# One decoder layer with a mixture of experts: GpSimd's expert loop without its outer branch, and a small copy moved from ScalarE's queue to SyncE's

## What is computed

```python
def hier_moe(h, w_rg, w_re, w_g, w_u, w_d):
    ...                                     # top-1 group of 4, then top-2 of its 8 experts
    order = jnp.argsort(flat_e)             # token-expert pairs, sorted by expert
    ...
    chunk_e = jnp.clip(jnp.searchsorted(pend, ...), 0, N_EXPERTS - 1)
    def expert_chunk(args):
        xc, e = args
        return (jax.nn.silu(xc @ w_g[e]) * (xc @ w_u[e])) @ w_d[e]
    ...
    out = jax.ops.segment_sum(ys.astype(jnp.float32) * slot_w[:, None], slot_tok, num_segments=n + 1)[:n]
```

## Time and profile before

| what | value |
|---|---|
| median of three runs | 1815.52 us (1813.52 to 1822.35) |
| the profiled execution: its time, its span | 1813.52 us, 1811.8 us |
| PE busy | 1439.0 us (79%) |
| PEld busy | 837.5 us (46%) |
| DVE busy | 664.2 us (37%) |
| ACT busy | 371.6 us (21%) |
| POOL busy | 192.8 us (11%) |
| moved by DMA | 336.98 MB, mean 186 GB/s |

### The profile page before, as it was taken

One profiled execution on the slowest core, in us unless ns is written; L12 is line 12 of the kernel. 1 busy time (PEld: TensorE's weight loads), 2 busy tenths in 40 slices (PEclk: granted clock), 3 DMA queues, 4 the chain that ended last, 5 costly groups with the idle time before them and its releaser, 6 DMA issues. The chain is left out here.

```text
span 1811.8 us, 22638 instructions
## 1 busy us (share of the span) xinstructions
PE 1439.0 (79%) x7436; PEld 837.5 (46%) x7436; DVE 664.2 (37%) x1324; ACT 371.6 (21%) x794; POOL 192.8 (11%) x348
## 2 busy tenths in 40 slices
PE   5999999448569978873369990699999999999960
PEld 4665454148535555552235540354454454454430
DVE  3002999941137766653512228011011011011007
ACT  4000011013125555552111110011111111111113
POOL 0000011136110000002300000111111111111111
PEclk7999999769858999996679995799999999999985
DMA  8300000076142000004441100899999999999927
GB/s 319 137 1 6 12 15 18 14 271 190 53 121 71 1 1 1 1 17 130 128 166 49 67 29 2 324 412 412 412 406 413 414 403 413 412 401 409 407 94 285
DMA packets 79756, 336.98 MB, mean 186 GB/s; under 512 B 9770, under 2 KB 41643, under 8 KB 61698
## 3 DMA queue, kind: packets, MB, share of 16 engines
q1 hardware_dynamic: 61866, 287.76, 40.6%
q0 software_dynamic: 15440, 47.30, 7.6%
q10 hardware_dynamic: 2384, 1.06, 0.2%
HBM read 311.20 MB, written 29.45 MB: 188 GB/s over the span
## 5 line engine op out<-in xcount | busy, mean ns | idle before, releaser
L1630 PE MATMUL ps<-arena 128*128 128x512 f32 x544 | 241.1, 600 | 0.0
L1630 PEld LDWEIGHTS ps<-arena 128*128 128x128 f32 x544 | 102.6, 191 | 137.5 <-issue 137.4
L311 PE MATMUL ps<-arena 128*128 128x512 f32 (+3 forms) x432 | 159.0, 528 | 1.3 <-DVE arena L439 1.3
L453 DVE SCALAR_TENSOR_TENSOR arena<-arena 128x1024 f32<-128x1024 f32 x120 | 144.3, 1278 | 0.3
L1331 PE MATMUL ps<-arena 128*128 128x512 f32 (+1 forms) x288 | 129.5, 603 | 15.5 <-DVE arena L1426 15.5
L1684 PE MATMUL ps<-arena 128*128 128x512 f32 x272 | 121.6, 600 | 3.8 <-DMA arena<-scratch_h,ints 3.8
L1638 PE MATMUL ps<-arena 128*64 128x256 f32 x1088 | 121.2, 380 | 0.0
L277 PE MATMUL ps<-arena 128*128 128x352 f32 x384 | 116.1, 465 | 0.4 <-ACT arena L340 0.4
L311 PEld LDWEIGHTS ps<-arena 128*128 128x128 f32 (+1 forms) x432 | 77.3, 180 | 80.8 <-issue 73.7
L935 ACT ACTIVATE arena<-ps,arena 128x640 f32<-128x640 f32 (+7 forms) x128 | 89.9, 702 | 119.9 <-DVE arena L1010 108.5
L848 PE MATMUL ps<-arena 128*128 128x128 f32 x528 | 82.8, 287 | 35.6 <-ACT arena L945 32.0
(11 more groups left out here) (357 smaller groups left out, 1551.4 us busy)
## 6 DMA issues: line engine op xcount, KB each, us to landing
arena<-in_w_gate SPq DMA_DIRECT2D x34, 2048.0 KB, 11.4
arena<-in_w_up SPq DMA_DIRECT2D x34, 2048.0 KB, 16.0
arena<-in_w_down SPq DMA_DIRECT2D x34, 2048.0 KB, 16.1
arena<-in_x_prompt SPq DMA_DIRECT2D x16, 512.0 KB, 6.7
arena<-in_cache_cmp POOLq DMA_DIRECT2D x64, 128.0 KB, 3.2
arena<-in_cache_cmp SPq DMA_DIRECT2D x64, 128.0 KB, 2.7
arena<-in_cache_sel SPq DMA_DIRECT2D x64, 128.0 KB, 2.1
arena<-scratch_y SPq DMA_DIRECT2D x16, 512.0 KB, 5.9
```

The source lines that it names most:

```text
L311: mm = pe.matmul(ps[:n, b + o // 512, 0:w], xT[:, k, t * P:t * P + n], w_tm[:, k, o:o + w], start=(k == 0), stop=(k == KT_ - 1))
L453: ins = dve.scalar_tensor_tensor(o, i, dw[:, c, j:j + 1], o, ALU.mult, ALU.add)
L1630: mm = pe.matmul(ps[:, bank, :], xgT_l[:, k, :], w[LARGE][:, k, :], start=(k == 0), stop=(k == KT_ - 1))
```

## The change

Three edits. The outer If of GpSimd's loop is gone, and the nine inner ones stand directly in the loop. GpSimd's two waits, for table_ready and for rows_ready, stand ahead of everything that it does in the block. The copy that doubles rows_f is issued by SP, ahead of the expert weights, instead of by ScalarE.

```diff
             n_rounds = round_count(pool)
-            pool.wait_ge(sem("table_ready"), 1)
             for s in range(2):
                 take_ids(s, 0, 0)
                 gather(s)
-            pool.wait_ge(sem("rows_ready"), 1)
             with pool.Fori(0, ROUNDS) as i:
+                for s in range(2):
+                    with pool.If(i < n_rounds):
+                        pool.wait_ge(sem(f"xg_in{s}"), i * 16 + 16)
+                    with pool.If(i < n_rounds):
+                        take_ids(s, i + 1, i + 1)
+                    with pool.If(i < n_rounds):
+                        gather(s)
+                        pool.wait_ge(sem(f"y_out{s}"), i * 16 + 16)
                 with pool.If(i < n_rounds):
-                    for s in range(2):
-                        with pool.If(i < n_rounds):
-                            pool.wait_ge(sem(f"xg_in{s}"), i * 16 + 16)
...
-                    with pool.If(i < n_rounds):
-                        take_rows(LARGE, out_l, i)
...
+                    take_rows(LARGE, out_l, i)
+                    pool.wait_ge(sem("y_l_act"), i + 2)
+                    pool.wait_ge(sem("y_l_dve"), i + 2)
+                with pool.If(i < n_rounds):
...
@@ expert block
             def _(sp):
                 o, w = const_at["lane"]
                 sp.dma_start(lane, a["consts"][:, o:o + w]).then_inc(sem("lane_in"), 16)
+                sp.wait_ge(sem("small_rows"), 1)
+                sp.dma_start(rows_f[HF:P, :], rows_f[0:HF, :]).then_inc(sem("rows_doubled"), 16)
                 expert_weights(sp)
...
-                act.wait_ge(sem("small_rows"), 1)
-                act.dma_start(rows_f[HF:P, :], rows_f[0:HF, :]).then_inc(sem("rows_doubled"), 16)
                 expert_silu(act)
...
             @block.gpsimd
             def _(pool):
+                pool.wait_ge(sem("table_ready"), 1)
+                pool.wait_ge(sem("rows_ready"), 1)
                 expert_rows(pool)
```

More of the change, by code:

```diff
@@ new lines, in expert_rows @@
+                with pool.If(i < n_rounds):
+                    pool.indirect_dma_start(scratch_y, bass.IndirectOffsetOnAxis(ap=out_l.bitcast(U32), axis=0),
+                                            y_l, None).then_inc(sem("y_out0"), 16)
+                    take_rows(SMALL, out_s, i)
+                    pool.wait_ge(sem("y_s_dve"), i + 2)
+                    pool.wait_ge(sem("y_out0"), i * 16 + 32)
+                with pool.If(i < n_rounds):
+                    pool.indirect_dma_start(scratch_y2, bass.IndirectOffsetOnAxis(ap=out_s.bitcast(U32), axis=0),
+                                            y_s, None).then_inc(sem("y_out1"), 16)
```

## The result

| | before | after |
|---|---|---|
| median of the runs | 1814.78 us (1813.52 to 1822.35) | 1844.18 us (1841.84 to 1846.19) |
| the profiled execution: its time, its span | 1813.52 us, 1811.8 us | 1846.09 us, 1844.5 us |

The ratio is 1.0156, with an interval of 1.0130 to 1.0183. The kernel became slower by 29.4 us, where 22 to 23 had been forecast. The forecast of 1838 us was 6 us short. The measured time lies above the 1834 to 1842 that the forecast called its own range, and 0.8 us under the upper end of the wider one, 1831 to 1845.

The account below looks back on a forecast made before the run. The prediction took the expert rounds to be bound by TensorE and the DMA engines almost equally, with serial stretches at both ends. It summed 1813.5 + 5 (head) + 19.2 (tail) = 1837.7, said 1838 us; own range 1834 to 1842, wider 1831 to 1845.

Parts of the forecast that it names:

- The skipping passes: GpSimd's loop: 15 passes without work take 120 more jumps of 0.16 us, 19.2 us, ends 15.0 and 23.4.
- Rival 1: GpSimd's skipping passes: a jump sits at its lower bound of 0.125 us, 15.0 us in all, 1833.5 us; 9%.
- rival 4: GpSimd's skips nearly free, all but 2 us of the head given back: 1820 to 1822 us; 4%.
- Nothing covers the tail: End of the expert block: GpSimd was already the last engine, so the whole 19.2 us shows.
- The DRAIN: End of the expert block: GpSimd's DRAIN follows its DMA count, waiting does not shorten it, it stays 5.94 us.
- rival 2: Block's end: the DRAIN finishes at about 1765 whenever begun, so 5.9 us of jumps lie under it, 1832 us; 8%.
- The first steps of the head: Before the rounds: weight stream 5.2 us late, gathers 4.0 to 4.5 late, TensorE's first round about 4 late.
- What of the head reaches the end: Expert rounds: the weight stream sets the pace, so its shift of 5.2 us, rounded to 5, is charged; ends 3 and 10.
- rival 3: Expert rounds: backlog some five rounds ahead, twelve rounds exposed to stalls, 4.5 us more, 1842 us; 12%.
- The sum: Whole kernel: 1813.5 + 5 (head) + 19.2 (tail) = 1837.7 us, given as 1838, 1.2% over the median.
- the straight test and ScalarE's issue: Working passes and ScalarE: one test per pass and one DMA issue fewer, costed at nothing; test 1 us if uncovered.

Follow-up runs that it names:

- e1: Kernel before with only GpSimd's outer If removed, the nine inner ones flat in the loop; 1832.93 us, ratio 1.0110.
- e5: Kernel before plus 30 small stores that GpSimd issues and waits for ahead of the gathers; 1812.7 us, one run.
- e7: Kernel before without GpSimd's DRAIN at the end of the expert block; 1815.34 us, ratio 0.9995.
- e2: Kernel before with only the 8 KB copy moved from ScalarE to SP, ahead of the weights; 1823.73 us, ratio 1.0049.
- e4: Kernel before with the copy on SP and GpSimd's two waits first, outer If kept; 1822.56 us, ratio 1.0038.
- e9: Kernel before with copy on SP, GpSimd's waits first, outer If kept, and the small expert's down weights loaded by half; 1815.16 us, ratio 0.9993.
- e3: Kernel before with only GpSimd's two waits moved ahead of everything, the copy still on ScalarE; 1829.49 us, ratio 1.0077.
- e6: Kernel before with GpSimd's outer If removed and all five engines' loops ending at the run-time round count; 1814.35 us, ratio 0.9966.
- e8: Kernel before with TensorE's six starting semaphore increments moved to the top of the block, ahead of its routing wait; 1811.05 us, ratio 0.9964.
- e10: Kernel before with a GpSimd DRAIN added in each working pass, behind the gathers; 1809.25 us, ratio 0.9953.
- e11: Kernel before with e8's early semaphores, e6's loop ends (outer If kept) and e10's DRAIN together; 1802.15 us, ratio 0.9911.

## Why the prediction was right, and where it was off

**The skipping passes: right.** 19.2 us were forecast from 120 jumps of 0.16; the trace gives 18.2 and 0.151. e1 shows them alone. Rival 1 (0.125) is out, and so is rival 4, which needed a jump below 0.05. Of the rule in the Trainium skill, Advanced Engine Details and Errata, Control Flow Timing, some 108 ns for a compare-and-branch, this case shows that it is too low for taken jumps one after the other on GpSimd: taken as an estimate, it would have made 13.0 us of what was 18.2.

**Nothing covers the tail: right.** GpSimd was the last at the barrier and stays it, with the other engines ready 18.8 us before it.

**The DRAIN: right.** It is 5.937 us in both, wherever it starts, so rival 2 is out. e5 and e7 show both sides of it: more DMAs make it longer, and leaving it out hands it on. But the prediction rested on two drains, and took from the one at L583, begun while its last load was still being issued, that transfers in flight make no difference. A row of the trace before speaks against that: 16 page loads, the last issued just ahead of the drain, cost 163 ns each, and the same drain took 2.6 to 3.1 us in the other profiles.

```profile
L786 POOLq DRAIN  x1: 2605/2605/2605, 510.3 to 510.3; - x1
```

Where all had landed, as at the end of the expert block, the count alone decides. That the forecast's drain was of this kind is why its 5.94 held.

**The first steps of the head: right, within 0.3 to 1.7 us.** From the block's start the marks of the prediction are 54.6 for the first gate load (measured 54.9), 57.5 for the first gather (56.8) and 74.1 for the first products (75.8). VectorE had the copy 1.9 us after its issue (1143.32 to 1145.21), where 2.4 were taken. The first products missed most, since the gathers' durations weren't kept: the second took 2.1 us longer, 15.9 instead of 13.8. How long it takes goes with the weights that are in flight beside it: 10.6 us in e2, where it goes out with the first of them, 13.8 before (5.9 us behind the first load) and 15.9 after (3.9 behind it). Why 3.9 is worse than 5.9 is not shown.

**What of the head reaches the end: the step that was mis-sized.** The prediction charged the stream's shift, 5 us, and the head measured 10.4 in after and 9.5 in e4 by the profile, 5.6 and 5.5 of them at TensorE's start and the rest in longer rounds. Its reason, that the stream sets the end, is borne out by e2 (TensorE 3 us early, end 6.4 late) and by e9 (a lighter stream and no wait at all); e3's profile shows the other side, a late start of TensorE that the rounds don't amplify. Its size was rival 3's, 5 + 4.5. That rival's mechanism is seen too, and stronger: stalls were to begin five rounds sooner, and the first gap of half a microsecond or more in TensorE's rounds is at 1226 instead of 1492, eight rounds sooner. The other profiles agree. Where the first weights go out 55 us into the block and the load is full (after, e2, e4), the first such gap comes at 127 to 169 us of the block and the down products wait 18.9 to 22.0 us for gathers. Where they go out at 49 to 50 or earlier (before, e1, e3, e5, e6, e7, e8, e10, e11), it comes at 270 us or later, in e5 never, and they wait 12.6 us at most. Rival 3 had 12%, and for the head it was the truer account.

Two things keep the 10.4 from being a sharp number. Kernels whose head is that of before ended TensorE's work at 656.2 (e5), 659.8 (e1), 661.9 (e7), 662.3 (before) and 663.6 (e10), with 0 to 10.2 us of waits for gathers. And the timed runs of e4 put the head at 7 us, between 2 and 12, which does not exclude the forecast's 5. What stays open is why one execution with the same head waits in its late rounds and another doesn't.

**The sum.** 24.2 us of changes were forecast and 32.7 measured in the profiles: 5.4 more in the head, 1.0 less in the tail, 3.6 in unchanged code, 0.5 in the rest. The timed medians are 29.4 us apart; e1 and e4 add up to 27 us by their ratios, 20 by their medians, and 28 by the tail of e1 and TensorE's end in e4. Nothing speaks against costing the straight test and ScalarE's issue at nothing, but the 1 us at stake is too small to be seen: in e1 the rounds with flat Ifs took 589.4 us, inside the 585.8 to 592.9 of the kernels with the old head.

## What to carry to other kernels

A loop whose bound is fixed while its work ends early is paid for behind the work, in jumps per skipping pass: leave such a pass with one jump, or let the loop end at the count. When two limits are nearly equal, price a late start by what it does to the fuller one, and expect up to twice the shift (here 5 us became about 10 in the profiles). GpSimd's DRAIN at a block's end is paid by the number of DMAs that it issued since its last one, and a DRAIN in a place where GpSimd waits anyway takes that off the path. A difference of 6 us between two profiles of this kernel proves nothing by itself.

## What the runs showed of the hardware beyond what was expected

- GpSimd's DRAIN at a block's end took 782 ns after 9 DMAs, 5937 after 72, 6672 after 81 and 8392 after 102, which is 82 to 87 ns for each one issued since the last DRAIN. All of them had landed when it began, in e5 the first ones more than 600 us earlier. With the 209 ns after 2 in e10, an estimate of 0.045 us plus 0.0818 for each DMA meets all five within 5 ns.
- While DMAs are still in flight the DRAIN is longer than that: 2605 ns for 16 page loads, and in e10's and e11's passes it ended 0.2 to 0.3 us after the last gather's landing, each time.
- An 8 KB copy within on-chip memory kept VectorE waiting 1.69 us when it stood ahead of the weights (after) and 8.0 to 8.6 beside them (e3, before).
- Taken jumps in a row cost GpSimd 0.151 us each.
- With 8% off a DMA load whose share was 1.01, TensorE's down products did not wait for a gather once in 17 rounds (e9), where the same head with the full load had 14 waits (e4).
- The same table products took TensorE 3.46 us of busy time with a granted clock of 0.99 and 6.16 with 0.50; which of the two an execution of this kernel gets moved the first gather by 2.7 us.
